# Turning attention weights head by head, and copying and weighing them bank by bank, in a two-layer decoder trunk

## The chip, the core and the metric

The kernel runs on one core of one Trainium2 chip. Five engines each run their own queue in order: PE (TensorE: matmuls, with weight loads listed apart as PEld), DVE (VectorE), ACT (ScalarE), POOL (GpSimd) and SP (SyncE, which issues most transfers here). They order themselves by semaphores: an instruction can raise one when it is done, and can wait for one to reach a value. The metric is the device time of one execution in microseconds (us), as the median of a few runs. In arithmetic everything is float32.

## The reference, cut to what matters

The model has two layers over 256 tokens of width 1024. Layer 0 mixes by "forgetting attention" (called fox in the kernel): 16 heads of 64, causal softmax with a bias from running sums of log-gates. Layer 1 mixes by native sparse attention (nsa): each of the 16 heads has a compressed, a selected and a window branch; at 256 tokens the selected and the window branch both see every earlier token, so each is one causal attention of its own. After each mixing comes a mixture of 64 experts.

```python
def block(args):                      # fox, one block of 128 queries
    qb, cq, bi = args
    logits = jnp.einsum('bqhd,bkhd->bhqk', qb, k, preferred_element_type=jnp.float32) * scale
    logits = logits + (cq.transpose(0, 2, 1)[..., None] - cum_k[:, :, None, :])
    ...
    p = jax.nn.softmax(jnp.where(mask[None, None], logits, -jnp.inf), axis=-1)
    return jnp.einsum('bhqk,bkhd->bqhd', p.astype(v.dtype), v)
...
o = gates[..., 0:1] * o_cmp + gates[..., 1:2] * o_sel + gates[..., 2:3] * o_win    # nsa
return o.reshape(B, S, hd) @ w_o
```

## The kernel before, in words

All large weights (512 MB of traffic in a run) stream through `ring`, 14 slots of 1 MB in SBUF, in one fixed order; SP issues a unit as soon as the slot it needs has been used by PE. So whenever PE works on something that uses no unit, as in both attentions, the ring fills up and the transfers stop until PE uses units again.

Attention is done in batches. A batch is one branch (`br`), one block of 128 queries (`t` = 0 or 1) and four heads (`g`). Block 0 sees 128 keys, block 1 sees 256. Fox has 8 batches: numbers 0 to 3 are narrow (`t` = 0), 4 to 7 wide (`t` = 1). Nsa has 16: 0 to 3 narrow and 4 to 7 wide for the first branch, 8 to 11 narrow and 12 to 15 wide for the second. Each batch goes through these steps:

- logits (PE, `pe_logits`, lines 643 and 648): four heads of 128 x 128 or 128 x 256 into two PSUM banks, which alternate between batches (banks 0, 1 and banks 2, 3).
- mask (DVE, lines 738 to 742): logits plus causal mask into one of three SBUF buffers `softmax_in`, the row maximum, and its negative.
- exponential (ACT, line 721): four ACTIVATEs, one for each head; each raises `probs_ready`.
- turn (PE, line 666): transposes of 128 x 128 through the identity into PSUM bank 4 (four of them, narrow) or banks 4 and 5 (eight, wide). Four transposes fill a bank, which is four heads of a narrow batch or two heads of a wide one.
- copy (ACT, line 713): one ACTIVATE copies the turned weights, 128 x 512 or 128 x 1024, from PSUM to `pT` in SBUF (shown as tile uT in the trace).
- weigh (PE, line 683): the turned weights of each head are the stationary operand, the values with a column of ones (128 x 65) stream; the result goes to bank 6 or 7.
- output (DVE, line 749 and on, 2061 for fox, 2215 to 2219 for nsa): reciprocal of the sum, multiplied into the heads.

The order is written out by hand on each engine. PE runs, for b = 0, 1, 2, ...: logits of b + 2, weigh of b - 1, turn of b; so logits stand between turn b - 1 and weigh b - 1 as long as there are logits left, and nothing stands between them in the last batches. ACT runs: exponentials of b, then copy of b - 1. DVE runs: mask of b + 2, then output of b - 1. There is one buffer `pT` and one pair of turned banks for all batches: copy b waits for weigh b - 1 (`heads_out`), turn b waits for copy b - 1 (`probsT_ready`). In fox one unit of the weights for the condition vectors ("ada", line 563) stands between turn 7 and weigh 7. In nsa three small steps are put in: the logits of the compressed branch ahead of turn 0 (line 1744), their transposes behind weigh 6 and 7 (line 1756), and the compressed heads ahead of weigh 14 (line 1767). DVE has the softmax of the compressed branch between its masks (lines 2182 to 2196).

## Time and profile before

| what | value |
|---|---|
| median of 3 runs | 1437.22 us (1435.86 to 1437.52) |
| profiled execution: its time | 1438.07 us |
| profiled execution: span in the trace | 1436.3 us |
| PE busy | 1381.5 us, 96% |
| DVE busy | 321.2 us, 22% |
| ACT busy | 266.1 us, 19% |
| DMA mean rate | 357 GB/s |
| fox attention (first logits to last weigh) | about 149 to 183 us |
| nsa attention (first turn to last weigh) | about 838 to 900 us |

The shares are averages over very different stages. Outside the two attentions PE is almost always busy; inside them it shares the work with DVE and ACT, and what counts is which of the three ends last at each batch.

### The profile page before, as it was taken

The page shows a single profiled execution, that of the slowest core. Times are in us where ns is not written, and L with a number is a line of the kernel's source. Part 1 is how long each engine was busy: PE and PEld are TensorE (multiplying, and loading weights), DVE is VectorE, ACT ScalarE, POOL GpSimd, SP SyncE. Part 2 cuts the span into 40 slices and gives each one's busy share as a digit, 9 for nine tenths or more (in the row PEclk, how much of TensorE's full clock was granted, in tenths as well). Part 3 has the DMA queues.
Part 4 walks back from the last instruction along what each step waited for, and adds up shares of the span by engine and source line. Part 5 has one row for each costly group of instructions (what it writes and reads, how often), then busy time and mean ns, then how long its engine had stood idle before and what let it go on. Part 6 is the DMA issues. An engine that isn't in the chain of part 4 may idle for free.

```text
span 1436.3 us, 20547 instructions
## 1 busy us (share of the span) xinstructions
PE 1381.5 (96%) x8361; PEld 788.8 (55%) x8361; DVE 321.2 (22%) x776; ACT 266.1 (19%) x519; POOL 31.6 (2%) x79
## 2 busy tenths in 40 slices
PE   5999899999999999999989988999999999999997
PEld 1777765555644444444458867854564444444442
DVE  1330523111111111111133477231110111111111
ACT  2211523110101111111133365231101111111110
POOL 5000000000100000000000000000010000000000
PEclk9999999999999999999999989999999999999999
DMA  9999289899999999999998600148999999999997
GB/s 376 413 421 421 115 338 407 351 389 420 364 420 421 420 421 420 421 422 420 420 418 332 233 30 1 61 174 363 421 374 404 421 420 421 420 420 421 421 420 289
DMA packets 71599, 512.30 MB, mean 357 GB/s; under 512 B 8240, under 2 KB 8432, under 8 KB 9552
## 3 DMA queue, kind: packets, MB, share of 16 engines
q1 hardware_dynamic: 70560, 509.64, 86.4%
q0 software_dynamic: 800, 1.25, 0.3%
q8 instruction: 68, 1.11, 0.3%
q14 instruction: 27, 0.22, 0.0%
q10 hardware_dynamic: 144, 0.08, 0.0%
HBM read 509.89 MB, written 1.05 MB: 356 GB/s over the span
## 4 chain that ended last, share of the span: by engine, by line
PE 89%; DMA 5%; DVE 3%; ACT 2%; issue 1%; SPq 0%; DVEq 0%; ACTq 0%
PE PS L925 23%; PE PS L915 13%; PE PS L933 12%; PE PS L536 12%; PE PS L949 11%; DMA ring<-in_w_exp 4%; PE PS L563 3%; PE PS L683 2%; PE PS L961 2%; DMA ring<-in_w_ada_units 1%; PE PS L1797 1%; PE PS L515 1%; PE PS L547 1%; PE PS L970 1%; PE PS L666 1%
## 5 line engine op out<-in xcount | busy, mean ns | idle before, releaser
L925 PE MATMUL PS<-ring,scratch 128*32 128x512 f32 (+2 forms) x2176 | 355.4, 597 | 7.3 <-DMA ring<-in_w_exp 5.9
L925 PEld LDWEIGHTS PS<-ring,scratch 128*32 128x32 f32 (+2 forms) x2176 | 111.5, 123 | 244.2 <-issue 242.3
L915 PEld LDWEIGHTS PS<-scratch,u 128*128 128x128 f32 x1600 | 183.0, 192 | 38.7 <-issue 36.8
L915 PE MATMUL PS<-scratch,u 128*128 128x128 f32 x1600 | 192.5, 278 | 1.4 <-ACT scratch L1149 1.4
L933 PE MATMUL PS<-ring,scratch 128*32 128x512 f32 (+2 forms) x1088 | 182.2, 596 | 2.3 <-DVE item_first_i L1265 1.2
L949 PE MATMUL PS<-scratch 128*128 128x512 f32 x384 | 172.7, 592 | 0.0
L1285 DVE TENSOR_TENSOR scratch<-PS,gate_row 128x512 f32<-128x512 f32 x100 | 69.2, 692 | 461.5 <-PE PS L933 461.5
L536 PE MATMUL PS<-ring,uT 128*128 128x256 f32 x672 | 149.3, 381 | 0.4 <-ACT uT L494 0.4
L1157 ACT ACTIVATE scratch<-PS 128x256 f32<-128x256 f32 x50 | 19.2, 384 | 675.2 <-PE PS L925 675.2
L536 PEld LDWEIGHTS PS<-ring,uT 128*128 128x128 f32 x672 | 126.1, 190 | 23.0 <-issue 6.5
L933 PEld LDWEIGHTS PS<-ring,scratch 128*32 128x32 f32 (+2 forms) x1088 | 52.6, 122 | 122.3 <-issue 120.6
L949 PEld LDWEIGHTS PS<-scratch 128*128 128x128 f32 x384 | 69.2, 190 | 68.9 <-issue 68.9
L1273 DVE TENSOR_TENSOR scratch<-scratch,PS 128x256 f32<-128x256 f32 x50 | 21.1, 422 | 331.6 <-ACT scratch L1157 331.6
L1149 ACT ACTIVATE scratch<-PS 128x512 f32<-128x512 f32 x100 | 59.7, 597 | 142.8 <-PE PS L915 142.8
L563 PE MATMUL PS<-ring,cond_cols 128*32 128x512 f32 x448 | 56.5, 626 | 14.3 <-DMA ring<-in_w_ada_units 14.3
L683 PE MATMUL PS<-scratch,uT 128*128 128x65 f32 x288 | 39.2, 289 | 9.7 <-ACT uT L713 9.4
L683 PEld LDWEIGHTS PS<-scratch,uT 128*128 128x128 f32 x288 | 35.9, 201 | 17.0 <-ACT uT L713 15.0
L721 ACT ACTIVATE scratch<-scratch,stats 128x128 f32<-128x128 f32 (+1 forms) x96 | 35.6, 443 | 15.2 <-DVE stats L742 15.2
L563 PEld LDWEIGHTS PS<-ring,cond_cols 128*32 128x32 f32 x448 | 12.1, 111 | 46.5 <-issue 32.4
L1162 ACT ACTIVATE scratch<-PS 128x512 f32<-128x512 f32 x50 | 29.6, 592 | 2.7 <-PE PS L943 2.7
L536 PE MATMUL PS<-ring,u 128*128 128x256 f32 x128 | 28.7, 381 | 0.0
L961 PE MATMUL PS<-uT,ring 128*128 128x256 f32 x128 | 28.3, 379 | 0.0
(332 smaller groups left out, 851.2 us busy)
## 6 DMA issues: line engine op xcount, KB each, us to landing
ring<-in_w_exp SPq DMA_DIRECT2D x384, 1024.0 KB, 16.6
ring<-in_w_ada_units SPq DMA_DIRECT2D x56, 1024.0 KB, 17.0
ring<-in_w_in_a_units SPq DMA_DIRECT2D x12, 1024.0 KB, 26.1
ring<-in_w_cmp_units SPq DMA_DIRECT2D x8, 1024.0 KB, 26.2
ring<-in_w_sh_units SPq DMA_DIRECT2D x6, 1024.0 KB, 13.6
ring<-in_w_kv_b_units SPq DMA_DIRECT2D x6, 1024.0 KB, 22.4
ring<-in_w_o_a_units SPq DMA_DIRECT2D x4, 1024.0 KB, 10.8
ring<-in_w_in_b_units SPq DMA_DIRECT2D x4, 1024.0 KB, 11.3
```

Source lines behind the costliest of these rows:

```text
L536: mm = pe_.matmul(PS[:, bank, t * UC:(t + 1) * UC], lhs[:, k, t * P:(t + 1) * P], w[:, k, :], start=(k == 0), stop=(k == KC - 1))
L563: mm = pe_.matmul(PS[32 * k:32 * k + 32, ADA, :], cond_cols[:, j % 2 * (KC // 2) + k, 31 - r:63 - r], w[:, k, :], start=(j == ada_units(st ...
L683: mm = pe_.matmul(PS[:, heads_bank(kind, b), hd * (DH + 1):(hd + 1) * (DH + 1)], pT[:, n * P:(n + 1) * P], values(br, kt, 4 * g + hd), sta ...
L721: eng.activation(p, p, ACT.Exp, bias=stats[:, b % 3, 4 + i:5 + i]).then_inc(probs_ready, 1)
L915: mm = pe_.matmul(PS[:, bank, i * w:(i + 1) * w], u[:, t, k * P:(k + 1) * P], hot[:, t, :], start=(t == 0), stop=(t == NT - 1))
L925: mm = pe_.matmul(PS[places, GU, :], x[:, kk, places], gate_and_up, start=(kk == 0), stop=(kk == KC - 1))
L933: mm = pe_.matmul(PS[places, Y0 + half, :], hT[:, j, places], down[:, j, half * 512:(half + 1) * 512], start=(j == 0), stop=(j == 1))
L949: mm = pe_.matmul(OUT[t][:, half * 512:(half + 1) * 512], hot_wT[0:rows, t * P:(t + 1) * P], y_rows[0:rows, half * 512:(half + 1) * 512], ...
L961: mm = pe_.matmul(PS[:, GATHER, i * SEQ:(i + 1) * SEQ], slot(AT[unit])[:, k, i * P:(i + 1) * P], uT[:, k, :], start=(k == 0), stop=(k == K ...
L1149: act.activation(x_pair[g % 2][:, 4 * half:4 * half + 4, :].rearrange("p k s -> p (k s)"), PS[:, gather_bank(g, half), :], ACT.Copy).then_ ...
L1162: act.activation(turned_sb[g % 2], PS[:, GU, :], ACT.Copy).then_inc(group_sem["turned_copied"], 1)
L1285: dve.tensor_tensor(y_rows[:, half * 512:(half + 1) * 512], PS[:, Y0 + half, :], gate_row[:, half * 512:(half + 1) * 512], ALU.mult).then_ ...
```

## The change

Three things are changed, all in the attention that both layers share. The exponentials are as before.

1. Turn: PE waits for each head's exponential by itself (one wait ahead of each head's transposes) where it waited for all four; and it raises `probs_turned` after each bank (every fourth transpose), where it did so once.
2. Copy: ACT copies one bank of 512 columns per ACTIVATE as soon as that bank is turned. A wide batch has two ACTIVATEs of 128 x 512 where it had one of 128 x 1024; a narrow batch still has one.
3. Weigh: PE waits for the first bank's copy ahead of head 0, and in a wide batch for the second bank's ahead of head 2, where it waited for all.

`banks_up_to` counts the banks of all batches before a given one, since the semaphores now count banks.

```diff
+        def banks_up_to(kind, b):
+            before_it = sum(t + 1 for br, t, g in attention_batches("fox")) if kind == "nsa" else 0
+            return before_it + sum(t + 1 for br, t, g in attention_batches(kind)[:b])
...
-                pe_.wait_ge(probs_ready, 4 * (b0 + b + 1))
                 if b >= 1:
-                    pe_.wait_ge(probsT_ready, b0 + b)
+                    pe_.wait_ge(probsT_ready, banks_up_to(kind, b))
                 p = softmax_in[b % 3]
                 for n in range(4 * (t + 1)):
+                    if n % (t + 1) == 0:
+                        pe_.wait_ge(probs_ready, 4 * (b0 + b) + n // (t + 1) + 1)
                     mm = pe_.transpose(PS[:, 4 + n // 4, (n % 4) * P:(n % 4 + 1) * P],
                                        p[:, n * P:(n + 1) * P], ident[:, :])
-                mm.then_inc(probs_turned, 1)
+                    if n % 4 == 3:
+                        mm.then_inc(probs_turned, 1)
...
-                pe_.wait_ge(probsT_ready, b0 + b + 1)
...
                 for i in range(4):
+                    if i * (t + 1) % 4 == 0:
+                        pe_.wait_ge(probsT_ready, banks_up_to(kind, b) + i * (t + 1) // 4 + 1)
...
-                n = 4 * width(batches[b][1])
-                eng.wait_ge(probs_turned, b0 + b + 1)
-                if b >= 1:
-
-                    eng.wait_ge(heads_out, b0 + b)
-                eng.activation(pT[:, 0:n], PS[:, 4:4 + n // 512, :].rearrange("p b c -> p (b c)"),
-                               ACT.Copy).then_inc(probsT_ready, 1)
+                for bank in range(batches[b][1] + 1):
+                    eng.wait_ge(probs_turned, banks_up_to(kind, b) + bank + 1)
+                    if b >= 1 and bank == 0:
+                        eng.wait_ge(heads_out, b0 + b)
+                    eng.activation(pT[:, bank * 512:(bank + 1) * 512], PS[:, 4 + bank, :], ACT.Copy
+                                   ).then_inc(probsT_ready, 1)
```

The order of the work on the engines is the same; waits and one ACTIVATE per wide batch are added. On PE at the end of fox, weigh 5 (L683) and turn 6 (L666) read before:

```order
L683 MATMUL PS<-scratch,uT 128x65 [waits heads_read,probsT_ready]
L683 MATMUL PS<-scratch,uT 128x65 x7
L666 MATMUL PS<-ident,scratch 128x128 [waits probsT_ready,probs_ready]
L666 MATMUL PS<-ident,scratch 128x128 x7
```

and now, at lines 691 and 672 of the changed kernel:

```order
L691 MATMUL PS<-scratch,uT 128x65 [waits probsT_ready,heads_read]
L691 MATMUL PS<-scratch,uT 128x65 x3
L691 MATMUL PS<-scratch,uT 128x65 [waits probsT_ready]
L691 MATMUL PS<-scratch,uT 128x65 x3
L672 MATMUL PS<-ident,scratch 128x128 [waits probs_ready,probsT_ready]
L672 MATMUL PS<-ident,scratch 128x128
L672 MATMUL PS<-ident,scratch 128x128 [waits probs_ready]
L672 MATMUL PS<-ident,scratch 128x128
L672 MATMUL PS<-ident,scratch 128x128 [waits probs_ready]
L672 MATMUL PS<-ident,scratch 128x128
L672 MATMUL PS<-ident,scratch 128x128 [waits probs_ready]
L672 MATMUL PS<-ident,scratch 128x128
```

A wide turn and weigh hold the same 16 matmuls, with four more that carry a wait. On ACT, copy 4 (L713) between the exponentials (L721) of batches 5 and 6 of fox reads before:

```order
L721 ACTIVATE scratch<-scratch,stats 128x256 [waits scores_shifted]
L721 ACTIVATE scratch<-scratch,stats 128x256 x3
L713 ACTIVATE uT<-PS 128x1024 [waits heads_out,probs_turned]
L721 ACTIVATE scratch<-scratch,stats 128x256 [waits scores_shifted]
L721 ACTIVATE scratch<-scratch,stats 128x256 x3
```

and now, at lines 728 and 720 of the changed kernel:

```order
L728 ACTIVATE scratch<-scratch,stats 128x256 [waits scores_shifted]
L728 ACTIVATE scratch<-scratch,stats 128x256 x3
L720 ACTIVATE uT<-PS 128x512 [waits heads_out,probs_turned]
L720 ACTIVATE uT<-PS 128x512 [waits probs_turned]
L728 ACTIVATE scratch<-scratch,stats 128x256 [waits scores_shifted]
L728 ACTIVATE scratch<-scratch,stats 128x256 x3
```

The copy stays behind the exponentials of the next batch; only its halves are apart.

## Rows read from the trace of the kernel before

**Rows 1.** Busy time by stretch: us, engines' busy time, PE clock, DMA share, GB/s.

```profile
core 0: us, PE busy (x) PEld busy (x) DVE busy (x) ACT busy (x) POOL busy (x), PEclk, DMA share, GB/s
170.00:185.00 15.00, 12.66 (x108) 9.65 (x107) 5.46 (x12) 4.75 (x8) 0.00 (x0) 1.00 0.16 63
240.00:700.00 460.00, 457.33 (x2721) 229.29 (x2720) 68.22 (x166) 56.14 (x102) 4.70 (x2) 1.00 0.99 408
854.00:860.00 6.00, 5.94 (x30) 5.61 (x32) 5.08 (x11) 2.24 (x6) 0.00 (x0) 0.50 0.00 0
880.00:891.00 11.00, 8.39 (x70) 7.55 (x71) 10.31 (x21) 6.31 (x13) 0.00 (x0) 1.00 0.00 1
960.00:1430.00 470.00, 462.43 (x2752) 227.21 (x2751) 63.49 (x136) 51.18 (x99) 4.70 (x2) 1.00 0.98 405
```

**Rows 2.** PE's idle time ahead of the turn's line 666: us, times.

```profile
  ACT scratch L721: 2.3, 2
```

**Rows 3.** Who waited for the copy, line 713: us, times.

```profile
  PEld PS L683: 15.0, 17
  PE PS L683: 9.4, 10
```

**Rows 4.** Timeline of fox: start, us, engine, line, count, idle before and releaser.

```profile
153.09 0.66 PE L666 MATMUL PS<-ident,scratch 128*128 128x128 f32 x4 [1.07 <-ACT scratch L721]
...
154.60 0.57 ACT L713 ACTIVATE uT<-PS 128x512 f32<-128x512 f32 x1
...
155.23 1.11 PE L683 MATMUL PS<-scratch,uT 128*128 128x65 f32 x8 [0.38 <-ACT uT L713]
...
160.22 0.60 ACT L713 ACTIVATE uT<-PS 128x512 f32<-128x512 f32 x1 [1.65 <-PE PS L666]
...
165.45 1.10 PE L683 MATMUL PS<-scratch,uT 128*128 128x65 f32 x8
...
166.39 1.04 PE L666 MATMUL PS<-ident,scratch 128*128 128x128 f32 x8
...
167.36 0.30 PEld L643 LDWEIGHTS PS<-scratch 64*128 64x128 f32 x4 [0.17 <-issue]
...
171.12 1.04 PE L666 MATMUL PS<-ident,scratch 128*128 128x128 f32 x8
...
172.20 1.02 ACT L713 ACTIVATE uT<-PS 128x1024 f32<-128x1024 f32 x1 [2.12 <-PE PS L666]
...
173.28 2.00 PE L683 MATMUL PS<-scratch,uT 128*128 128x65 f32 x16 [1.11 <-ACT uT L713]
...
177.27 2.00 PE L683 MATMUL PS<-scratch,uT 128*128 128x65 f32 x16 [1.11 <-ACT uT L713]
...
180.08 1.06 PE L563 MATMUL PS<-ring,cond_cols 128*32 128x512 f32 x8
...
181.27 2.00 PE L683 MATMUL PS<-scratch,uT 128*128 128x65 f32 x16
```

**Rows 5.** Timeline of nsa, the same columns.

```profile
851.40 1.71 ACT L721 ACTIVATE scratch<-scratch,stats 128x256 f32<-128x256 f32 x4 [3.01 <-DVE stats L742]
...
853.01 1.00 ACT L713 ACTIVATE uT<-PS 128x1024 f32<-128x1024 f32 x1
...
854.06 3.67 PE L683 MATMUL PS<-scratch,uT 128*128 128x65 f32 x16 [2.57 <-ACT uT L713]
...
864.55 2.00 PE L683 MATMUL PS<-scratch,uT 128*128 128x65 f32 x16 [0.47 <-ACT uT L713]
...
868.64 2.00 PE L683 MATMUL PS<-scratch,uT 128*128 128x65 f32 x16 [0.47 <-ACT uT L713]
...
870.86 0.18 DVE L749 RECIPROCAL stats<-PS 128x4 f32<-128x4 f32 x1 [0.96 <-PE PS L1756]
...
887.48 1.00 ACT L713 ACTIVATE uT<-PS 128x1024 f32<-128x1024 f32 x1
...
888.53 2.00 PE L683 MATMUL PS<-scratch,uT 128*128 128x65 f32 x16 [1.17 <-ACT uT L713]
```

More of the change, by code:

```diff
@@ L735, in mask @@
                 if b >= 3:
-                    eng.wait_ge(probs_turned, b0 + b - 2)
+                    eng.wait_ge(probs_turned, banks_up_to(kind, b - 2))
                 s = softmax_in[b % 3][:, 0:4 * w].rearrange("p (i w) -> p i w", i=4)
```

## The prediction

> **What bounds the kernel now.** I read the busy time by stretch first, because a gain in attention only counts if the stretches behind it pass it on. In the long expert stages PE is busy 457.33 of 460 us and 462.43 of 470 us, with the DMA engines busy 0.99 and 0.98 [rows 1]. The reader is to see two streams that both run full. Whether PE or the transfers set the pace there hardly matters here: in the attentions the ring is full and the transfers stand (0.16 and 0.00 busy in the attention stretches of [rows 1]), so they start again when PE next frees a slot. If PE leaves an attention x us earlier, the transfers restart x us earlier too, and both streams move by x. So I take a gain at the end of either attention at full value.
>
> Then I read who waited for the operations that change. The gain that head-by-head turning aims at is small: PE stood ahead of the turn for the exponentials 2.3 us in two entries [rows 2], which are one wait seen on its matmul row and on its weight-load row: the 1.07 us ahead of turn 0 of fox [rows 4]. The wait for the copy is larger: 9.4 us of PE's idle time [rows 3]. Of these, 1.11 us each stand ahead of weigh 5 and weigh 6 of fox, and 2.57, 0.47, 0.47 and 1.17 us ahead of weigh 4, 6, 7 and 13 of nsa [rows 4, 5]. So the question is which of these waits is the copy's own length (which halving it shortens) and which is something that the copy itself had waited for.
>
> **Turning head by head.** Turn 0 of fox could begin about 0.9 us earlier and follow the exponentials. But weigh 0 waits for copy 0, and ACT runs copy 0 at 154.60 only because the exponentials of batch 1 are ahead of it in its queue; PE had finished turn 0 at 153.75 (153.09 + 0.66) [rows 4]. A turn that ends earlier meets the same copy at 154.60 and the same weigh at 155.23. So I cost the gain at nothing in fox. In nsa turn 0 does not wait for exponentials in [rows 2] at all. After that no turn waits for them. This part gives 0.
>
> **Copy and weigh bank by bank, fox.** Batches 4 to 7 are wide. Ahead of weigh 4 stand the logits of batch 7 (from 167.36), and they cover the copy; no wait, no gain. For weigh 5 nothing covers it: the turn starts at 171.12, the copy at 172.20 and runs 1.02 us, the weigh at 173.28 [rows 4]. Now the first bank is complete after four transposes; four take 0.66 us in the row of turn 0, of which 0.05 is its own start after a wait, so 0.61 [rows 4]. The first copy starts 0.04 us later (the turn's 1.04 us and the copy at 172.20 give that distance), at 171.77. A 128x512 copy takes 0.57 or 0.60 us [rows 4]; I take 0.60, and 0.06 from its end to the weigh (172.20 + 1.02 = 173.22 against 173.28). Weigh 5 starts at 172.43 and not 173.28: 0.85 us. Its second half needs the second copy; that is done by about 172.95, while heads 0 and 1 take 1.00 us of the weigh's 2.00, until 173.4. No new wait. Weigh 6 is the same once more: 0.85 us. Ahead of weigh 7 stands the ada unit from 180.08 to 181.14, and the weigh starts at 181.27 [rows 4]; only the last 0.13 us or so are the copy's, and I take 0.15. Fox: 0.85 + 0.85 + 0.15 = 1.85 us.
>
> **The same in nsa.** Three places. (a) Weigh 4. The wait of 2.57 us is mostly not the copy's: ACT was in the exponentials of batch 5 from 851.40 (it had waited 3.01 us for DVE's statistics), and the copy follows them at 853.01 [rows 5]. The first half ends 0.57 us after its start and not 1.00, so weigh 4 gains 0.43. (b) Weigh 5, 6, 7. PE is what everyone waits for from here until DVE takes over at 870.86 (DVE had waited 0.96 us for PE there). Weigh 6 and 7 each lose the 0.47 us of idle time, since the first half of their copy falls under the logits between; weigh 5 started 0.1 us after the logits and gives at most that. With (a): 0.43 + 0.47 + 0.47 = 1.37, and that much earlier DVE starts its chain at 870.86. From there to about 890 DVE is busy 10.31 of 11 us [rows 1], its own length sets the pace, and a faster copy only changes who waits. (c) Weigh 13, after the last logits. Its copy at 887.48 is behind exponentials that are behind DVE; half of it is 0.43 us sooner [rows 5]. From weigh 13 to the end of the attention PE waits for no copy, so this goes through. Nsa: 1.37 + 0.43 = 1.80 us.
>
> **What it adds.** On ACT two 128x512 copies take the place of one of 128x1024, in 12 wide batches. Two starts on ACT overlap: copy 0 of fox ended at 155.17 (154.60 + 0.57) as a whole in the row, and 853.01 lies 0.10 us ahead of the end of its exponentials at 853.11 (851.40 + 1.71) [rows 5]. So the pair takes 0.57 + 0.57 - 0.10 = 1.04 against 1.00: 0.04 us, hidden because the second half is not waited for. If that cover goes it costs 0.04 to 0.15 for each of 12, so 1.8 us at most. On PE there are 84 more waits (3 for each of 24 turns, 1 for each of 12 wide weighs) and 12 more increments; about 43 of the waits lie where PE sets the end (turns 2 to 7 and weighs 4 to 7 of fox, turns 5 to 7 and weighs 5 to 7 of nsa, and the last ones). Nearly all are fulfilled when PE reaches them. What does a fulfilled wait cost? The turn behind weigh 3 of fox carries two waits and follows an increment, and it starts 0.94 us after a weigh of eight matmuls whose busy time is 1.10 (165.45 to 166.39) [rows 4]: no gap. So below, nothing. Above, by the only crossing that shows one, turn to logits (166.39 + 1.04 = 167.43 against 167.36, where weight loads pause about 0.1 us while the shape changes from 128 to 64 rows), 0.09 each, or 3.9 us. The first row has the same shape on both sides, as the added waits have; I take 0.
>
> The Trainium skill speaks against the added increments: its page "TensorE: Matmul & The Clock Gate", section "The cost: per-tile semaphore tail", has increments on matmuls serialize at about 26 ns each and advises one on the last. By that, 12 more are an estimated 0.3 us worse. The crossing just read bears an increment and shows no such step.
>
> **Sum.** 1.85 + 1.80 - 0 = 3.65 us. The profiled execution took 1438.07 us, of which 1436.3 are the span; it would become 1434.4. It lay 0.85 above the median of the runs, so against the median of 1437.22 I forecast 1433.6 us. The bounds of my own terms: 3.65 + 0.3 (0.57 for 0.60, the 0.1 at weigh 5) = 4.0, 3.65 - 1.8 = 1.85 with the ACT cost at its worst, and 3.65 - 3.9 = -0.25 with the added waits at 0.09 us each.
>
> **Rivals.**
> (A) As above, 1433.6. Chance 0.55.
> (B) The clock of PE goes better. In 854 to 860 us its granted clock was 0.50, that is 1.2 in place of 2.4 GHz [rows 1], right behind the idle time of 2.57 us; weigh 4 took 3.67 us there against 2.00 for its like, and a turn of 1.04 us would take some 0.9 more at half the clock. With a shorter wait ahead of it and other positions in time, this dip may not come. Weigh 4 gives 1.67, turn 5 some 0.9; DVE would then be the next limit a little sooner, so I count 2.3: 1431.3. For it: the gap shrinks to 2.1 us; against: it is still there. Chance 0.12. The skill's same page, section "What's actually happening", has the clock follow PE's recent activity and the position of a dip vary from run to run; the rows show only one run's dips.
> (C) A dip more, where PE now idles beside DVE (880 to 891: busy 8.39 of 11). A weigh and a turn at the low clock cost 2.5 us: 1436.1. Chance 0.08.
> (D) The gain of one attention is lost later, because something behind it does not move with it. The candidate is the expert stage: DMA is 0.98 to 0.99 busy, and if data set its pace by a start that does not follow PE, 1.8 us go: 1435.4. For: both streams run full. Against: transfers stood nearly still in both attentions. Chance 0.13.
> (E) Fulfilled waits are not free. The decision point is 3.65 / 43 = 0.085 us a wait. If each costs 0.17 us, which is how long PE's weight loads pause ahead of the waiting logits at 167.36 [rows 4], 43 cost 7.3 us: 1440.9, slower. The place is every turn and weigh from 156 to 183 and 857 to 900 us. Against it is the weigh-to-turn crossing. Chance 0.05, and 0.07 is left for smaller mixtures that end between 1434.5 and 1437.5.
>
> **How the numbers follow.** A measurement of this kernel tells about 0.2% from no change, which is 2.9 us: faster means below 1434.35. A gives 0.51 of its 0.55 to faster, B all of its 0.12: 0.63. C, D, the rest of A and the mixtures give 0.32 to no change, E 0.05 to slower. The range reaches from B's end to C: 1430.8 to 1436.4.
>
> **What would show it.** In the profile after: PE's wait for the copy, 9.4 us, falls to about 6, with 0.25 us ahead of weigh 5 and 6 of fox in place of 1.11, none ahead of weigh 6 and 7 of nsa, and about 2.1 ahead of weigh 4. The wait ahead of fox's turn 0 is split over its four transposes while weigh 0 still starts where it did, with the copy behind the exponentials of batch 1. From fox's weigh 0 at 155.23 to the end of weigh 7 at 183.27 it is 28.0 us now and should be 26.2; from nsa's weigh 0 to its last weigh it should be 1.8 us less. The weigh-to-turn crossings stay at 0.94 us for a narrow batch. I am wrong if a wide turn or weigh takes more than its 1.04 or 2.00 us at the full clock, if PE waits for the second bank inside a weigh, or if both attentions shorten and the total does not.

## The result, and the profile after

The changed kernel took 1432.13 us in the median of 20 runs (1429.81 to 1438.64), and the kernel before, beside it, 1438.34 us (20 runs, 1435.52 to 1450.51): ratio 0.9934, 95% interval 0.9916 to 0.9953. A second measurement gave 0.9963 (0.9942 to 0.9983; medians 1433.55 and 1440.71). So it is faster, by 5 to 9.5 us by the two ratios, where 3.65 us were forecast; the medians are 6.2 and 7.2 us apart, the means 7.5 and 6.2. The profiled execution took 1433.73 us against 1438.07.

Both kernels have a spread that three runs did not show, and the number above can't be read without it: over 144 runs the kernel before lies between 1435.5 and 1452.4 us, with runs gathered near 1436, 1441, 1445 and 1450.

The attentions first. The timeline of fox in the changed kernel (columns as in [rows 4]; turn is L672, weigh L691, copy L720, exponential L728):

```profile
150.68 1.21 PE L672 MATMUL PS<-ident,scratch 128*128 128x128 f32 x4 [0.20 <-ACT scratch L728]
...
153.06 0.58 ACT L720 ACTIVATE uT<-PS 128x512 f32<-128x512 f32 x1
...
153.69 1.11 PE L691 MATMUL PS<-scratch,uT 128*128 128x65 f32 x8 [0.71 <-ACT uT L720]
...
163.91 1.11 PE L691 MATMUL PS<-scratch,uT 128*128 128x65 f32 x8
...
164.85 1.04 PE L672 MATMUL PS<-ident,scratch 128*128 128x128 f32 x8
...
169.59 1.04 PE L672 MATMUL PS<-ident,scratch 128*128 128x128 f32 x8
...
170.23 1.09 ACT L720 ACTIVATE uT<-PS 128x512 f32<-128x512 f32 x2 [1.73 <-PE PS L672]
...
170.97 1.97 PE L691 MATMUL PS<-scratch,uT 128*128 128x65 f32 x16 [0.34 <-ACT uT L720]
...
174.17 1.97 PE L691 MATMUL PS<-scratch,uT 128*128 128x65 f32 x16 [0.34 <-ACT uT L720]
...
176.95 1.06 PE L563 MATMUL PS<-ring,cond_cols 128*32 128x512 f32 x8
...
177.94 2.00 PE L691 MATMUL PS<-scratch,uT 128*128 128x65 f32 x16
```

The reader is to see three things. Turn 0 now takes 1.21 us instead of 0.66, since it follows the exponentials head by head, and weigh 0 starts as before right behind copy 0: the turn's early start bought nothing. The copy of a wide batch starts 0.64 us after its turn instead of 1.08, and the idle time ahead of weigh 5 and 6 is 0.34 instead of 1.11. From the start of weigh 0 to the start of the last matmul of weigh 7 it is 25.98 us, against 27.76 in the kernel before; to the end of that matmul it is 26.25 against 28.04, where 26.2 was forecast. The crossing from a narrow weigh to the next turn is 0.94 us (163.91 to 164.85), as in [rows 4].

The same in nsa:

```profile
849.52 1.70 ACT L728 ACTIVATE scratch<-scratch,stats 128x256 f32<-128x256 f32 x4 [3.00 <-DVE stats L749]
...
851.13 1.05 ACT L720 ACTIVATE uT<-PS 128x512 f32<-128x512 f32 x2
...
851.85 3.65 PE L691 MATMUL PS<-scratch,uT 128*128 128x65 f32 x16 [2.17 <-ACT uT L720]
...
861.75 2.00 PE L691 MATMUL PS<-scratch,uT 128*128 128x65 f32 x16
...
865.30 2.00 PE L691 MATMUL PS<-scratch,uT 128*128 128x65 f32 x16
...
867.52 0.18 DVE L756 RECIPROCAL stats<-PS 128x4 f32<-128x4 f32 x1 [0.43 <-PE PS L1763]
...
884.84 1.97 PE L691 MATMUL PS<-scratch,uT 128*128 128x65 f32 x16 [1.21 <-ACT uT L720]
```

These answer [rows 5]: 2.17 us instead of 2.57 ahead of weigh 4, nothing ahead of weigh 6 and 7 (0.47 each before), and the exponentials stand behind DVE as they did. Weigh 4 again ran at half the clock (3.65 us). Who waited for the copy (us, times), answering [rows 3]:

```profile
  PE PS L691: 6.2, 7
  PEld PS L691: 0.9, 1
```

The busy time by stretch, answering [rows 1], shows that the expert stages are what they were (457.33 us busy of 460), and that in 854 to 860 us the granted clock was 0.64 rather than 0.50, since the low stretch lies earlier:

```profile
170.00:185.00 15.00, 14.32 (x126) 10.26 (x124) 6.78 (x25) 7.23 (x14) 0.00 (x0) 1.00 0.37 136
240.00:700.00 460.00, 457.33 (x2727) 230.01 (x2726) 67.27 (x162) 55.59 (x103) 4.69 (x2) 1.00 0.99 408
854.00:860.00 6.00, 6.00 (x39) 5.44 (x39) 4.83 (x9) 3.60 (x9) 0.00 (x0) 0.64 0.01 1
```

So the waits went much as forecast. The question left was where the rest of the gain came from. The two profiled executions alone can't say it. Of the 4.33 us between their spans, 1.54 lie ahead of weigh 0 of fox, where only the waits of turn 0 differ; fox gives 1.79 and nsa 0.94, the stage between the attentions takes 0.55 more and the stage behind nsa 0.62 less. The parts outside fox move with low-clock stretches, which lie elsewhere in each execution.

### The profile page after: what moved, and what is told of

Same layout as the page of the kernel before. It is cut to its first block, busy times and chain, and to the rows that moved or that the text cites. A ratio compares the mean times of both kernels' runs of the same rounds, so it can differ in the third digit from the quotient of the medians.

```text
span 1432.0 us, 20559 instructions
## 1 busy us (share of the span) xinstructions
PE 1383.3 (97%) x8361; PEld 792.2 (55%) x8361; DVE 321.0 (22%) x776; ACT 267.2 (19%) x531; POOL 31.5 (2%) x79
## 3 DMA queue, kind: packets, MB, share of 16 engines
q8 instruction: 68, 1.11, 0.3%
HBM read 509.89 MB, written 1.05 MB: 357 GB/s over the span
## 4 chain that ended last, share of the span: by engine, by line
PE 90%; DMA 5%; DVE 3%; ACT 1%; issue 1%; SPq 0%; DVEq 0%; ACTq 0%
PE PS L932 23%; PE PS L922 13%; PE PS L940 12%; PE PS L536 12%; PE PS L956 11%; DMA ring<-in_w_exp 4%; PE PS L563 3%; PE PS L691 2%; PE PS L968 2%; PE PS L1804 1%; DMA ring<-in_w_ada_units 1%; PE PS L515 1%; PE PS L547 1%; PE PS L977 1%; PE PS L648 1%; PE PS L672 1%
## 5 line engine op out<-in xcount | busy, mean ns | idle before, releaser
L691 PE MATMUL PS<-scratch,uT 128*128 128x65 f32 x288 | 39.5, 290 | 6.4 <-ACT uT L720 6.2
L691 PEld LDWEIGHTS PS<-scratch,uT 128*128 128x128 f32 x288 | 36.4, 203 | 13.4 <-issue 11.3
L728 ACT ACTIVATE scratch<-scratch,stats 128x128 f32<-128x128 f32 (+1 forms) x96 | 35.6, 444 | 15.3 <-DVE stats L749 15.3
```

Source lines behind the costliest of these rows:

```text
L691: mm = pe_.matmul(PS[:, heads_bank(kind, b), hd * (DH + 1):(hd + 1) * (DH + 1)], pT[:, n * P:(n + 1) * P], values(br, kt, 4 * g + hd), sta ...
L728: eng.activation(p, p, ACT.Exp, bias=stats[:, b % 3, 4 + i:5 + i]).then_inc(probs_ready, 1)
```

## The experiments

My theory after the result: the bank-by-bank copy is worth about 3.7 us by its waits, the head-by-head turning nothing, and the remainder is TensorE's clock, which falls to half for some microseconds in the attentions, at places and for lengths that differ between executions and, on average, between the kernels. The rival: fewer waits are worth more than I read, by something that every execution has.

### One half of the change at a time

Heads alone (turn waits for each head, whole copy), from the kernel before:

```diff
-                pe_.wait_ge(probs_ready, 4 * (b0 + b + 1))
 ...
                 for n in range(4 * (t + 1)):
+                    if n % (t + 1) == 0:
+                        pe_.wait_ge(probs_ready, 4 * (b0 + b) + n // (t + 1) + 1)
```

> Only the turning head by head: PE waits for each head's exponential by itself; the copy and the weighing as before. By the sum in the prediction 0 us: weigh 0 meets the same copy behind the next exponentials. Ratio 0.999 to 1.001 under theory W. Rival H (this part carries the gain that the sum lacks, by keeping PE active through the exponentials): 2 us or more less, ratio under 0.9986.

Banks alone is the changed kernel with one wait for all four exponentials ahead of the turn's loop, in place of the wait for each head.

> Only the copy and the weighing bank by bank: PE waits once for all four exponentials ahead of a turn. Theory W: the whole gain, 3.65 us, ratio 0.9970 to 0.9980. Rival H: less than the changed kernel by 2 us or more.

Both kernels themselves ran once more beside these:

> The kernel before, unchanged, against itself, to see how far its runs spread and what PE's mean granted clock is in each. The measured ratio of the change was 0.9934 (0.9916 to 0.9953), some 9 us, where the two profiled executions differ by 4.3 us. Theory W (only the shortened waits gain, 3.65 us; the rest of the measured ratio is runs of before that happened to have more low-clock stretches): ratio 1.000, within 0.998 to 1.002, and the time of each run follows its mean clock, about 1 us for 0.001. Rival S (the runs of before are slow for a cause without a trace in the clock): the times spread by 10 us at equal clock.

> The changed kernel once more. Theory W: 3.65 us less than before at equal mean clock, ratio 0.9970 to 0.9980. Rival C (the shorter waits also spare low-clock stretches, at a typical run and not by luck): again 0.993 to 0.996, and a mean clock that is higher than that of before by 0.001 to 0.003.

Measured, all beside the same 30 runs of the kernel before (median 1440.71): the kernel before again 0.9989 (0.9964 to 1.0014), heads alone 0.9999 (0.9973 to 1.0025), banks alone 0.9948 (0.9924 to 0.9972, 7 runs), the changed kernel 0.9963 (0.9942 to 0.9983). Heads alone is nothing, and from fox's weigh 0 to 7 it takes 27.76 us, the time of the kernel before to the hundredth, with 24 waits more in it (72 in both attentions). Banks alone is all of the change as far as these intervals can tell; fox takes 25.97 us with it.

The trace of heads alone gave the first sight of what else there is. Its execution took 1441.6 us. Its attention stretch by windows (columns as in [rows 1]), and its last weighs:

```profile
867.00:884.60 17.60, 15.72 (x131) 13.04 (x131) 15.54 (x34) 10.42 (x26) 0.00 (x0) 1.00 0.00 1
884.60:901.70 17.10, 15.99 (x90) 15.03 (x89) 6.84 (x17) 4.83 (x9) 0.00 (x0) 0.50 0.00 1
```

```profile
887.26 3.67 PE L684 MATMUL PS<-scratch,uT 128*128 128x65 f32 x16 [1.11 <-ACT uT L714]
...
896.28 3.68 PE L684 MATMUL PS<-scratch,uT 128*128 128x65 f32 x16
```

For 17.1 us TensorE had the half clock, and a weigh took 3.67 us for 2.00. From the mask of batch 15 to the last weigh matmul it took 19.68 us, against 12.24 in the profile of the kernel before: 7.4 us by one stretch of low clock, which is twice the forecast gain.

### Every trace read at the same marks

The stretches at 1.2 GHz inside the attentions (start and length, us), and the times between marks, each from start to start. "Fox" is weigh 0 to the last matmul of weigh 7; "nsa" is its first exponential to its last weigh matmul; "tail" is the mask of batch 15 to that matmul. "Third extra", "filled" and the other kernels are told below.

| kernel | total | fox | nsa | tail | low clock in the attentions |
|---|---|---|---|---|---|
| before | 1438.07 | 27.76 | 63.26 | 12.24 | 839.7: 3.4; 853.3: 6.8 |
| before, again | 1436.43 | 27.76 | 62.96 | 12.24 | 853.5: 6.8 |
| before, first extra | 1436.5 | 27.76 | 62.86 | 12.25 | 853.1: 6.8 |
| before, second extra | 1436.19 | 27.76 | 62.97 | 12.25 | 853.6: 6.8 |
| before, third extra | 1436.85 | 27.77 | 62.97 | 12.25 | 838.9: 13.7 |
| heads alone | 1441.6 | 27.76 | 69.07 | 19.68 | 836.8: 6.8; 884.6: 17.1 |
| changed | 1433.73 | 25.98 | 62.33 | 11.88 | 834.4: 6.8; 851.5: 6.8 |
| changed, again | 1435.42 | 25.97 | 64.17 | 16.70 | 837.2: 10.2; 885.0: 10.2 |
| banks alone | 1436.75 | 25.97 | 65.81 | 18.34 | 835.3: 10.2; 883.1: 13.7 |
| banks in fox only | 1441.4 | 25.97 | 70.81 | 21.40 | 837.1: 10.2; 881.5: 20.5 |
| banks in nsa only | 1433.31 | 27.94 | 60.93 | 11.88 | 838.8: 13.7 |
| before, filled in nsa | 1439.96 | 31.91 | 62.11 | 12.50 | 176.3: 10.2 (in fox) |
| changed, filled in nsa | 1432.47 | 25.97 | 60.81 | 12.49 | 838.5: 3.4 |
| before, both filled | 1436.25 | 27.83 | 60.50 | 12.25 | none |
| changed, both filled | 1430.66 | 25.85 | 60.80 | 11.82 | 836.4: 10.2 |
| before, filled in fox | 1440.31 | 27.82 | 68.15 | 17.14 | 839.0: 13.7; 890.2: 10.2 |
| whole weigh | 1440.53 | 26.95 | 66.54 | 16.42 | 853.0: 6.8; 883.7: 10.2 |
| copy first | 1428.72 | 25.97 | 56.72 | 10.48 | 851.1: 3.4 |
| copy first, filled | 1426.38 | 25.84 | 57.32 | 11.14 | none |
| copy first, filled, again | 1426.02 | 25.85 | 57.30 | 11.15 | none |

Fox reads the same in every kernel without banks in it (27.76 to 27.94), and in every one with them (25.84 to 25.98), except where a low stretch lies in it and except in the whole weigh, which has only a part of the change. Nsa varies by 4 to 8 us within one kind of kernel, and its column follows the last one. But it goes by where a stretch lies and not only by its length. In the kernel before, 13.7 us at 838.9 and 6.8 us at 853 give the same nsa, 62.97 us: PE at half the clock reached weigh 4 so late that its wait of 2.57 us was gone (0.05 us were left).

Three more profiles of the kernel before:

> One more profile of the kernel before. Its 121 timed runs lie in groups: half from 1435.5 to 1439, others near 1441, 1445 and 1450. Theory C: a run near 1441 has either the 10.2 us at half clock at the end of fox (fox 4.15 us longer) or the stretch of 17 us from 885 us in nsa (mask 15 to weigh 15 19.7 in place of 12.2 us); one near 1450 has both or longer ones; one near 1436 has neither. Rival: a slow run without a low-clock stretch in an attention.

> As for the first of these three looks at the kernel before: the time of the profiled run is told by which of the two attentions has a low-clock stretch in it.

> As for the first of these three looks at the kernel before: the time of the profiled run is told by which of the two attentions has a low-clock stretch in it.

They took 1436.5, 1436.19 and 1436.85 us: none fell near 1445 or 1450, so I have no trace of such an execution, and what it holds is not shown. The third turned out useful in another way: it has nearly the same 13.7 us of low clock, at 838.9, as banks in nsa only (below, 838.8), so in nsa the two differ by their waits alone.

### The banks in one attention only

```diff
+        def banks(kind, t):
+            return t + 1 if kind == "nsa" else 1
 ...
-                    if n % (t + 1) == 0:
+                    if kind == "nsa" and n % (t + 1) == 0:
 ...
             def copy(b):
-                for bank in range(batches[b][1] + 1):
+                n = width(batches[b][1]) // (P * banks(kind, batches[b][1]))
+                for bank in range(banks(kind, batches[b][1])):
```

This is cut to what matters: the waits of turn and weigh follow the same rule. The other kernel has "fox" in the two places.

> The change in nsa alone; fox as before. By the sum 1.80 us from the waits. Theory C: all that goes beyond 3.65 us belongs to nsa, since fox shows no low-clock stretch in any profile; so the fastest runs are 3.5 to 5 us under the fastest of before (1435.5), around 1431. Theory W: 1.8 us, 1433.7.

> The change in fox alone; nsa as before. From the waits 1.85 us. Theory C: the stretches that fox can have go too, those of nsa stay; the fastest at 1433.7 (1435.5 less 1.85), no run above 1447 where before has 9 of 97 above 1450, mean 3 to 4 us under that of before (1440.3). Theory W: the same spread as before, 1.85 us lower.

The traces part the gain. Of the kernel before (third extra profile), and then of banks in nsa only, the low stretch and the weighs of batches 5 to 7 and 12:

```profile
838.90:852.60 13.70, 13.70 (x60) 10.30 (x58) 11.47 (x26) 7.00 (x19) 0.00 (x0) 0.50 0.01 2
```

```profile
859.71 2.00 PE L683 MATMUL PS<-scratch,uT 128*128 128x65 f32 x16 [0.47 <-ACT uT L713]
863.70 2.00 PE L683 MATMUL PS<-scratch,uT 128*128 128x65 f32 x16 [0.47 <-ACT uT L713]
867.79 2.00 PE L683 MATMUL PS<-scratch,uT 128*128 128x65 f32 x16 [0.47 <-ACT uT L713]
...
883.62 2.00 PE L683 MATMUL PS<-scratch,uT 128*128 128x65 f32 x16 [1.43 <-ACT uT L713]
```

```profile
838.80:852.50 13.70, 13.70 (x60) 10.69 (x60) 11.64 (x26) 6.68 (x19) 0.00 (x0) 0.50 0.01 2
```

```profile
859.18 2.00 PE L696 MATMUL PS<-scratch,uT 128*128 128x65 f32 x16
862.63 2.00 PE L696 MATMUL PS<-scratch,uT 128*128 128x65 f32 x16
866.19 2.00 PE L696 MATMUL PS<-scratch,uT 128*128 128x65 f32 x16
...
881.68 1.97 PE L696 MATMUL PS<-scratch,uT 128*128 128x65 f32 x16 [1.03 <-ACT uT L726]
```

The reader is to see that the stretch is the same in both, that the three waits of 0.47 are gone, and that the wait ahead of weigh 12 is 0.40 shorter. Nsa takes 62.97 - 60.93 = 2.04 us less, where I had forecast 1.80: 1.5 of it between weigh 4 and weigh 8, 0.43 between weigh 11 and weigh 12. Weigh 4 gives nothing here, since it does not wait in either. In fox it is 27.76 - 25.98 = 1.78, forecast 1.85. Together the waits give 3.8 us.

The runs tell another story: nsa only 0.9996 (0.9962 to 1.0031), with four runs at 1432.8 to 1434.2 and seven at 1442 to 1450; fox only 0.9999 (0.9972 to 1.0026), with 11 of 12 above 1438. In the mean each half gives next to nothing (1440.8 and 1441.1 us, against 1440.7 and 1441.4 for the runs of the kernel before beside them), while both together give 6 to 8. The forecasts of theory C (low-clock stretches that follow the waits for the copy) failed here, 1431 for the fastest run of nsa only (measured 1432.8) and a mean 3 to 4 us lower for fox only (0.3 lower); none of fox only's 12 runs was above 1447, as it said. Two waits that are each shown to be shorter don't add like that; the table shows what eats them in the one traced execution of fox only: 20.5 us of low clock at 881.5 and a tail of 21.40 us in place of 12.24. That an edit which shifts an attention in time also shifts how often such a stretch falls into it would fit, but no run tests it. Why these two kernels meet it more often stays open.

### How much is waits, how much is clock

Each run lists its mean granted clock. Over 112 runs of the kernel before (those beside the experiments), time follows it with a correlation of -0.95, at 0.99 us for each 0.001; over 32 runs of the changed kernel, with -0.86 and 0.98 us. The means are 1441.1 us at 0.9881 and 1433.3 us at 0.9914. At an equal clock of 0.990 the two lines stand at 1439.2 and 1434.6. So of 7.8 us (6.5 to 9.1) between the means, 4.6 (3.8 to 5.4) are there at the same clock and 3.2 go with the clock. (Intervals by resampling the runs.) The 3.8 of the traces lie at the lower end of that interval.

This split is an estimate, for two reasons. The runs of the two kernels were in part on different chips; with those that ran beside each other the means are 6.2 and 7.5 us apart. And equal time does not need equal clock: two executions of the kernel before took 1436.5 us at 0.994 and 1436.85 at 0.989, because the second one's low stretch fell where PE would have waited.

The traces show a further part outside the attentions. From the end of fox to the first exponential of nsa it is 652.7 to 652.9 us in all seven traces with fox as it was and unfilled, each with a low stretch of 3.4 us at 716 to 717. It is 651.8 to 652.2 us in the five traces with banks in fox that have no stretch there, and 653.5 in the changed kernel's first, with one at 735.5.

Whether the clock is a cause or a companion was tested by filling PE's idle time with matmuls of no use, ahead of the weighs that wait (they write unused columns of a bank):

```diff
+                if (kind, b) in FILL:
+                    for _ in range(FILL[kind, b]):
+                        pe_.matmul(PS[:, heads_bank(kind, b), 4 * (DH + 1):384], ident[:, :], causal[:, 0:384 - 4 * (DH + 1)],
+                                   start=True, stop=True)
```

In the kernel before, the wait for the copy moves behind these matmuls.

First in nsa only (14 ahead of weigh 4, 7 each ahead of 12 and 13), in both kernels:

> The kernel before with idle time of PE in nsa filled: 14 extra matmuls of 128x124 ahead of weigh 4 and 7 each ahead of weigh 12 and 13, into unused columns, while PE waits for the copy there (2.57, 1.43 and 1.17 us). They add no step that anyone waits for. Theory C (the copy waits cost twice: the waiting itself, and low-clock stretches of PE that follow it; the gain beyond 3.65 us is from those): the 6.8 us at half clock from 853 us are gone, nsa's mask 4 to mask 15 takes 41.2 us as in the profile of the heads-only kernel, which had no such stretch, and not 43.8; the fastest runs are 2 to 3 us under the fastest of before, ratio 0.997 to 0.9985. Theory W (waits alone, 3.65 us, and chance): no faster than before, 0.999 to 1.001.

> The changed kernel with the same extra matmuls at the same places. Theory C: against the filled kernel before only the waits' own 3.65 us remain, so the medians of the two filled kernels are 3 to 4.5 us apart, and this one is no more than 1.5 us faster than the changed kernel at the fastest runs. Theory W: the same distance, but from a filled kernel that is no faster than before.

Measured: before 1439.01 us (1434.71 to 1442.11; 0.9972, 0.9944 to 0.9999), changed 1433.77 (0.994, 0.9914 to 0.9967). The runs above 1443, a quarter of the kernel before's, are gone; but 8 of 12 gathered near 1439, and the fastest is only 0.8 us under the fastest of before (2 to 3 were forecast). The mean of the changed kernel did not fall (1433.8, unfilled 1433.3); its runs only drew together. The medians are 5.2 us apart, forecast 3 to 4.5. The trace gives one reason: the filled nsa no longer has a low stretch, and fox has one.

```profile
156.00:176.00 20.00, 18.53 (x155) 15.79 (x155) 15.11 (x26) 12.97 (x30) 0.00 (x0) 1.00 0.00 1
176.00:186.50 10.50, 9.30 (x45) 6.93 (x44) 1.21 (x4) 2.05 (x2) 0.00 (x0) 0.51 0.01 2
```

```profile
176.22 1.87 PE L666 MATMUL PS<-ident,scratch 128*128 128x128 f32 x8
...
179.29 3.65 PE L687 MATMUL PS<-scratch,uT 128*128 128x65 f32 x16 [1.20 <-ACT uT L718]
...
182.74 1.91 PE L666 MATMUL PS<-ident,scratch 128*128 128x128 f32 x8
```

The clock falls at 176.3, behind the wait ahead of weigh 5 (1.21 us in this trace, 1.11 in [rows 4]), though PE was busy 18.53 of the 20 us ahead of it. Fox takes 31.91 us: 4.15 more. A second reason is that 14 extra matmuls are too many: from weigh 3 to weigh 4 it is 6.98 us in both filled kernels, where it was 5.61 in the kernel before and 5.19 in the changed one, so they do stand on the path. The change takes 0.77 us off the waits ahead of weigh 5 and 6. So I filled fox as well (4 matmuls ahead of weigh 5 and 6, one each where the change had shortened the wait; 7, 4 and 4 in nsa):

> The kernel before with PE's idle time filled in both attentions: 4 extra matmuls of 128x124 ahead of weigh 5 and of weigh 6 of fox (idle 1.11 us each), and in nsa 7 ahead of weigh 4, 4 ahead of weigh 12 and 13 each. The profile of the kernel filled in nsa alone had a half-clock stretch of 10.2 us in the end of fox, where the attention took 4.15 us more than in every other profile of before. Theory C (low-clock stretches that follow waits for the copy, in fox and nsa, are what goes beyond 3.65 us): no stretch in fox, none from 853 or 885 us on, and the times lie close together, all within about 4 us and near 1435, with none above 1440; ratio 0.996 to 0.998. Theory W (chance): they spread over 15 us as those of before do.

> The changed kernel filled at the same places, with 1 in place of 4 in fox, where only 0.34 us are idle, and the same in nsa. With the low-clock stretches out of both kernels, theory C gives what the waits alone are worth: 3 to 4.5 us between the medians of the two filled kernels, with this one near 1431.5. Rival G (the waits themselves are worth 6 us): 5 us or more between them.

Before 1435.86 us (0.9956, 0.9933 to 0.998), 11 of 12 at or below 1436.8, within 6.9 us (4 were forecast); changed 1430.64 (0.992, 0.9891 to 0.9948; 7 runs). The filled fox of the kernel before, by the same windows as above:

```profile
156.00:176.00 20.00, 19.54 (x163) 16.83 (x164) 15.08 (x26) 12.94 (x30) 0.00 (x0) 1.00 0.01 2
176.00:186.50 10.50, 10.07 (x86) 7.33 (x86) 3.17 (x8) 2.05 (x2) 0.00 (x0) 1.00 0.33 105
```

What a low stretch costs is shown here. Filling saves no wait (fox 27.83 us against 27.76; weigh 3 to weigh 4 of nsa 5.53 against 5.61), but from weigh 4 to weigh 8 of nsa it is 15.59 us without the stretch at 853 and 17.81 to 17.98 with it. The kernel before is 5.8 us faster in the mean than unfilled (1435.6 against 1441.4 for its 24 runs beside it): work of no use, put into idle time, removed the runs above 1440 and raised the mean clock to 0.9937. So the low clock costs time, and with less idle time in both attentions it comes less often. That the idle time as such makes the stretches is the likeliest reading but not shown: other edits of this kernel changed how often they come too (banks in one attention only), and the same matmuls at a place where PE does not wait were not run.

Between the medians of the two filled kernels 5.2 us are left, more than the 3.8 of the waits and above the 5 at which rival G was to hold. The traces do not put it in the waits either. Of the 5.6 us between the two spans 1.98 are fox, and nsa takes 0.31 us more in the changed kernel: it has a low stretch at 836.4, and its 7 extra matmuls ahead of weigh 4 meet no wait any more (weigh 3 to weigh 4 takes 4.64 us, against 2.98 in the changed kernel with a like stretch). The other 3.9 us lie outside the attentions: 1.15 ahead of fox, 1.06 between them and 1.72 behind nsa, where this trace of the kernel before has stretches at 739 and 934 us which the changed one lacks. So this pair does not measure what the waits are worth.

Fox filled alone, in the kernel before:

> The kernel before with PE's idle time filled in fox alone: 4 extra matmuls ahead of weigh 5 and of weigh 6. With theory C the fox stretch (4.15 us) is gone and that of nsa stays possible: no run near 1450 (before has 13 of 121 above 1449), while runs of 1440 to 1446 remain, and with the change in fox alone as a guide (11 of 12 above 1438) they may be the most. If runs near 1450 remain, the slowest group is not the two stretches together.

1445.08 us (1.0002, 0.9973 to 1.0032): none near 1450, but seven of 12 at 1444.8 to 1447.2. Its trace has fox at 27.82 us without a low stretch, and nsa at 68.15 with two (839.0: 13.7; 890.2: 10.2). This agrees with the group at 1450 being executions with stretches in both attentions at once, but it is weak: 18 of 144 runs of the kernel before are above 1449, so 12 runs without one would come by chance once in five times, and no such execution was traced.

### Is the gain in the weigh or in the copy?

```diff
-                    if i * (t + 1) % 4 == 0:
-                        pe_.wait_ge(probsT_ready, banks_up_to(kind, b) + i * (t + 1) // 4 + 1)
+                    if i == 0:
+                        pe_.wait_ge(probsT_ready, banks_up_to(kind, b + 1))
```

> The changed kernel, but each weigh waits for both of its banks; turning and copying are by bank. It separates the two halves of the gain at weigh 5 of fox: with the copy of bank 0 begun under the turn of bank 1, both copies end about 0.65 us after the turn, so weigh 5 starts some 0.45 us sooner than before and 0.5 us later than in the changed kernel. From weigh 0 to the last weigh fox takes 27.0 us, between 27.76 (before) and 25.98 (changed). If the overlap of copy and turn is worth nothing: 27.7.

One run: fox 26.95 us, between 27.76 and 25.98, with

```profile
170.90 1.04 PE L672 MATMUL PS<-ident,scratch 128*128 128x128 f32 x8
...
172.78 1.97 PE L691 MATMUL PS<-scratch,uT 128*128 128x65 f32 x16 [0.83 <-ACT uT L720]
```

Starting the first copy after half the turn gives 0.8 of the 1.8 us, and starting the weigh after half the copy the other 1.0. At weigh 5 it is 0.28 us (1.88 us from the start of the turn in place of 2.16), where 0.45 was forecast; the sum over weigh 5 to 7 came out as forecast. (Its 1440.53 us hold low stretches at 853.0 and 883.7 in nsa, and say nothing on the edit.)

### A version that beats both

In nsa, weigh 4 waits because copy 4 stands behind exponentials which wait for DVE. The copy can go first:

```diff
+                if b >= 1:
+                    copy(b - 1)
                 eng.wait_ge(scores_shifted, b0 + b + 1)
                 for i in range(4):
                     ...
-                if b >= 1:
-                    copy(b - 1)
```

> The changed kernel with ACT's order turned round: copy of batch b - 1 ahead of the exponentials of batch b. In nsa the waits ahead of weigh 4, 12 and 13 are for a copy that stands behind exponentials that wait for DVE; so with the copy first they go. Theory C expects the wait of 2.2 us ahead of weigh 4 to be under 0.5, the next low-clock stretch there gone, and 2 to 4 us less than the changed kernel, about 1428. Rival (the exponentials are then late instead, since ACT waits for the turn before it starts them): turns wait 0.3 us or more each in fox's batches 2 to 5, and the kernel is not faster than the changed one.

> The changed kernel with the copy ahead of the exponentials, and one extra matmul ahead of fox's weigh 5 and 6, three ahead of nsa's weigh 12 and 13. The copy-first kernel had the fastest profile (1428.7, with 14.7 us from nsa's mask 15 to the end of weigh 15 gone down to 10.5 from 11.9), but its times spread from 1428.7 to 1439.0. Theory C: the extra matmuls keep the clock up in the last batches and the slow runs go; median 1429 to 1431.5, the best of all kernels. Rival (the extra matmuls stand on the path by now): median 1432 or more.

> The fastest kernel so far once more, to have its ratio on another chip: median 1426 to 1428, all within 4 us, ratio 0.987 to 0.993.

Copy first: 1433.11 us (0.9945, 0.9915 to 0.9974), lowest 1428.72; nsa 56.72 us in that execution. In the median it is no faster than the changed kernel (1432.13 and 1433.55), where 1428 was forecast: the wait ahead of weigh 4 is 1.20 us, now for DVE, and not under 0.5, and a low stretch of 3.4 us follows it. Then with one useless matmul ahead of weigh 5 and 6 of fox and three ahead of 12 and 13 of nsa: 1426.75 (0.9899, 0.9866 to 0.9931; 6 runs), and, again, 1428.9 (0.993, 0.9894 to 0.9965; 12 runs, of which 8 lie within 1426.0 to 1429.5 and 4 at 1439.4 to 1439.8), which misses the forecast of 1426 to 1428 with all runs within 4 us. The first trace has no wait for the copy left in nsa's wide batches; what PE waits for there is DVE (1.20 us ahead of weigh 4, and these):

```profile
855.28 2.00 PE L695 MATMUL PS<-scratch,uT 128*128 128x65 f32 x16
858.84 2.00 PE L695 MATMUL PS<-scratch,uT 128*128 128x65 f32 x16
...
874.12 0.93 PE L687 MATMUL PS<-causal,ident 128*128 128x124 f32 x6 [1.00 <-DVE scratch L2229]
874.89 1.90 PE L695 MATMUL PS<-scratch,uT 128*128 128x65 f32 x16
...
878.17 0.93 PE L687 MATMUL PS<-causal,ident 128*128 128x124 f32 x6 [0.50 <-DVE scratch L2229]
878.93 1.90 PE L695 MATMUL PS<-scratch,uT 128*128 128x65 f32 x16
```

Over its 18 runs the mean is 1430.2 us, 3 us under the changed kernel's 1433.3 and level with the changed kernel filled in both attentions (1430.6, 7 runs); its fastest run, 1426.02, is the fastest of all. Four of the 18 runs still lie some 11 us above the others.

## Why the prediction was right or wrong

**Head by head: 0.** Right. Heads alone gave 0.9999 and fox to the hundredth. The copy behind the exponentials of batch 1 keeps weigh 0 where it was, 0.63 us behind the start of copy 0 in both kernels.

**Banks in fox: 1.85.** Measured 1.78. The idle time ahead of weigh 5 and 6 is 0.34 rather than 0.25: from the start of the turn to that of the copy it is 0.64 us, as forecast (0.65), and from the copy to the weigh 0.74 instead of 0.66.

**Banks in nsa: 1.80.** Measured 2.04, between two traces with the same low stretch, but not from the terms of the sum. That pair has no wait ahead of weigh 4, so term (a), 0.43, is not in it. In its place weigh 5 has a wait that goes, like those of 6 and 7, and the three give about 0.5 us each; I had left weigh 5 out, which hardly waits (0.10 us) in the profile I read. Term (a) can be read in the changed kernel's first profile: 2.17 us ahead of weigh 4 instead of 2.57, so 0.40. Term (c), 0.43, is right: weigh 12 and weigh 13 both start 0.43 us sooner behind weigh 11. That the total lies so near the forecast is in part luck.

**Full value behind the attentions.** The expert stage is as busy as before (457.33 of 460 us). Rival D (one attention's gain lost later) finds nothing in its favour: at equal clock the runs differ by 4.6, not by 1.8, and the stage between the attentions is not longer with banks in fox than without, unless a low stretch lies in it.

**Fulfilled waits and increments: 0.** Right. Rival E is refuted: of the 72 more waits in heads alone 24 lie in fox, and they cost 0.00 us there; eight transposes take 1.04 us with and without the added increment, and the crossing is 0.94 in both. The Trainium skill's page "TensorE: Matmul & The Clock Gate", section "The cost: per-tile semaphore tail", would have 26 ns for each of 12. Nothing of it is seen in the turn, which is read to 0.01 us and takes the increment midway; the page speaks of increments that complete together. The ACT pair of copies takes 1.05 to 1.09 against 1.00 to 1.02, hidden as said.

**The clock.** This is the step that failed. The sum has no term for the clock: it takes PE's granted clock to be the same after as before. I priced a change in it only as rival B, one dip that may not come, a saving of 2.3 us with a chance of 0.12, and as rival C, one dip more at 2.5 us. It is neither: the low stretches are a distribution, of 3.4 to 20.5 us each inside the attentions, at about 2.7 us of cost at weigh 4, 4.15 in fox, and 4.8 to 9.2 in the tail of nsa. They put the kernel before 5.6 us above its own fastest run in the mean. With the whole change the mean granted clock rises from 0.9881 to 0.9914, and that share, an estimated 3.2 of 7.8 us, was missing from the sum. What in the change raises it is not shown: each half alone left it lower (0.9874 in fox only, 0.9869 in nsa only). From three runs within 1.7 us of each other, I took the spread to be small; 112 runs have a standard deviation of 4.9 us. The Trainium skill's same page, section "What's actually happening", says that the clock follows PE's recent activity; I cited it and let it change only one stretch. The traces agree in direction: with PE's idle time filled in both attentions, the kernel before has no stretch there. The varying position that I took from it is said there of the clock's rise when matmuls begin; that stretches inside a kernel move from run to run is shown by the table (839.7 and 853.3, 853.5, or 838.9, for the same kernel).

So the forecast's direction held, its sum of waits (3.65) is within 0.2 us of what the traces show (3.8), and its total fell short, as far as the runs tell by the clock.

What stays open: the groups at 1445 and 1450 us were never traced; nor was the changed kernel at its 1429 to 1431, so that it lacks the 2.7 us stretch at weigh 4 there is only consistent with the gap of 6.8 us between the two lowest runs (3.8 + 2.7 = 6.5); why each half of the change alone meets low stretches more often, and the whole change less; whether idle time makes them, or any shift in time would; and how the 5.2 us between the kernels filled in both attentions are made up over many runs.

## What to carry to other kernels

Halving a copy between a producer and a consumer on the same engine pays what it looks like it pays in the timeline, if both sides are split: here, over weigh 5 to 7 of fox, 0.8 us for starting the copy sooner and 1.0 for starting the consumer sooner. Splitting the side that nothing waits for pays nothing. Before a change of a few microseconds is forecast or judged, see how the runs spread and compare traces at equal marks and equal low-clock stretches; three runs that agree may all be from one group. Add up two traces stage by stage before their difference is put down to the edit: here 1.5 of 4.3 us lay ahead of fox's first weigh. Where PE idles for about a microsecond every few, between small matmuls, look whether the granted clock falls there; a few useless matmuls in both attentions took 5.8 us off the mean here, and in only one of them 2.2 us (nsa) or nothing (fox). Too many of them stand on the path themselves.

## What the runs showed of the hardware that I had not expected

TensorE fell to 1.2 GHz though it had been busy 15.72 of the 17.6 us ahead (heads alone) and 18.53 of the 20 us ahead (before, filled in nsa), with no single idle time over 1.43 us; it stayed low for 17.1 and 10.2 us. It can stay low while PE is busy all through, as in the changed kernel's second profile:

```profile
885.00:895.20 10.20, 10.20 (x64) 9.64 (x63) 3.23 (x10) 2.83 (x7) 0.00 (x0) 0.50 0.01 2
```

A busy share read at the low clock is no sign of health: the same weigh takes 3.65 to 3.68 us there in place of 2.00. What a low stretch costs goes by what PE would else have waited for: in the kernel before, 13.7 us at 838.9 and 6.8 us at 853 left nsa at the same 62.97 us. And a wait that is fulfilled when PE reaches it costs nothing that the 24 added in fox could show.
